# A hybrid encoder block on one core: wide half-K matmuls for queries and values, and a new order of weight chunks

## The chip, the cores and the metric

The kernel runs on one core of a Trainium2 chip. The metric is the device time of one execution, in microseconds (us). PE is TensorE, ACT ScalarE, DVE VectorE, POOL GpSimd and SP SyncE, which issues most DMAs. Each engine works through its own list of instructions in order and waits on semaphores.

## The reference

One layer on x of 2048 tokens by 1024, float32:

```python
h = rmsnorm(x, norm1_w)
qa, ka, va, qb, fb, ib, gb = split(h @ w_in)   # 512, 128, 128, 512, 512, 512, 512 columns
ya = sliding-window attention of qa, ka, va    # 8 query heads, 2 key heads, QK norm, partial rotary, sinks
yb = gated linear recurrence of qb, fb, ib     # 4 heads of 128, chunks of 64, rmsnorm, times silu(gb)
x  = x + concat(ya, yb) @ w_out
x  = x + (silu(h2 @ w_gate) * (h2 @ w_up)) @ w_down    # h2 = rmsnorm(x, norm2_w)
```

## The kernel before

Phase A computes everything up to `x + concat(ya, yb) @ w_out`; the feed-forward phase behind it (from about 840 us) isn't touched. A product of float32 operands is made of three passes (`three_passes`, L350 to L352): both operands are split into a high part in the matmul's format and the rest, and PE computes high x high, high x low and low x high.

Phase A takes the tokens in NB = 4 blocks of 512. For each block PE goes through twelve weight chunks (`CHUNKS`). A chunk is 1 MB (0.5 for F0 and F1): SP loads it into `w_stage`, ACT writes its high part (`split_hi`, L814), DVE the low part (`split_lo`, L1188). There are two buffers of each, used in turn, so a chunk is split while PE works on the one before. Heads of F, Q and G (names in `FIRST_HEAD`) are computed transposed, with the weights stationary and 512 tokens as moving columns, 24 matmuls a head. KV, QA0, QA1, I01 and I23 have the activations stationary and 256 weight columns moving, in four groups of 128 tokens, 24 matmuls a group. G's heads are cut in halves, `part` and `proj`. All of them write the banks `pj` in turn, and ACT reads each bank before its second next group.

Between the groups stand all other steps of the block, in an order written by hand (`block_steps`). Each entry `after(chunk, group, steps)` places steps behind a group, and every engine does its own share of each step in that one order, so a step that waits on an engine holds all that stands behind it there. The steps: `qn1`, `qn2` norm and rotary of queries and keys; `qT`, `kT` their transposes; `sc` scores of 128 tokens; `sm1` maximum (DVE) and exponentials (ACT) of one head group; `sm2` the division (DVE); `pt` transposes the probabilities on PE, and ACT copies them; `pv` times the values. For each of four recurrent heads: `ha` the log gate, `hb` its running sums (DVE) and then five exponentials (ACT), `hc` products (DVE), `att`, `kt` and `ds` matmuls and transposes with an ACT or DVE reading of their bank, `o` the output, `on1`, `on2` its norm, `yt` its transpose. `sq`, `n1a`, `n1b`, `xT` load, normalise and transpose the next block's x. The transposes of `qT`, `pt`, `kt`, `ds` and `yt` share two banks `tr`, used in turn: each waits until the bank's last content but one has been read. `sc` of t > 0 waits for the exponentials of t - 1.

`first_steps` are the two split steps of the next chunk. They stand ahead of group 0 of a chunk with heads and behind group 0 of the others, unless `block_steps` has placed them itself. What is left of the last heads of a block is done within KV and QA0 of the next (`LAST_HEAD`), and behind the last block within the output products (`out_steps`).

## Time and profile before

| | |
|---|---|
| median of 3 runs | 2134.61 us (2134.19 to 2135.76) |
| the profiled execution | 2135.83 us, of which the span from the first to the last instruction is 2134.0 |
| mean granted TensorE clock | 0.997 |
| PE busy in the span | 2099.1 us |

The profile is of one execution. A wait names the engine and the line that released it. Durations of neighbouring matmuls overlap, so the time of one in a stream is read from start to start. In a timeline the number in brackets is the engine's idle time before that row.

### The profile page before, as it was taken

The numbers are of one execution on the slowest core, as the hardware profiler recorded it, in microseconds if no ns is written. First come the engines' busy times: TensorE is split into PE (matmuls) and PEld (weight loads), VectorE is DVE, ScalarE is ACT, GpSimd is POOL, SyncE is SP. The second block draws the span as 40 slices with busy tenths as digits, with TensorE's granted clock in tenths as the row PEclk, the third lists the DMA queues.
The fourth block names the chain that finished last, engine by engine and source line by source line (L and its number), as shares of the span: only waits on it lengthen the run. The fifth ranks groups of instructions, "written<-read, shape, count | busy, mean of one in ns | idle before, by whom it ended". The sixth has DMA issues, their size and how long they took to land.

```text
span 2134.0 us, 28560 instructions
## 1 busy us (share of the span) xinstructions
PE 2099.1 (98%) x11128; PEld 1771.7 (83%) x11128; DVE 1377.9 (65%) x2034; ACT 886.0 (42%) x1490; POOL 105.5 (5%) x108
## 2 busy tenths in 40 slices
...
GB/s 280 130 75 124 165 80 85 199 80 104 134 86 216 204 263 203 163 133 145 152 158 173 96 146 168 217 143 178 151 144 178 170 253 185 205 179 167 181 134 90
DMA packets 176662, 338.10 MB, mean 158 GB/s; under 512 B 10448, under 2 KB 105936, under 8 KB 161552
## 3 DMA queue, kind: packets, MB, share of 16 engines
...
## 4 chain that ended last, share of the span: by engine, by line
PE 60%; DVE 0%; DVEq 0%; ACT 0%; issue 0%
PE b_bank_A L351 4%; PE b_bank_A L350 4%; PE b_bank_A L352 4%; PE b_bank_C L351 4%; PE b_bank_B L351 4%; PE b_bank_C L352 4%; PE b_bank_B L350 4%; PE b_bank_C L350 4%; PE b_bank_B L352 4%; PE b_hx_bank L1932 3%; PE b_hx_bank L1930 3%; PE b_hx_bank L1931 3%; PE b_bank_D L350 2%; PE b_bank_D L351 2%; PE b_bank_D L352 2%; PE b_hx_bank L1875 1%
## 5 line engine op out<-in xcount | busy, mean ns | idle before, releaser
L1816 ACT ACTIVATE b_s_hi<-b_s_stage 128x1408 fp32r<-128x1408 f32 x56 | 77.4, 1383 | 300.2 <-PE b_hx_bank L1932 143.7
L350 PE MATMUL a_pj<-a_w_hi,a_hT_hi 128*128 128x256 f32 x640 | 185.7, 290 | 1.5 <-DVE a_hT_lo L1202 1.5
L351 PE MATMUL a_pj<-a_w_lo,a_hT_hi 128*128 128x256 f32 x640 | 181.0, 283 | 0.0
L352 PE MATMUL a_pj<-a_w_hi,a_hT_lo 128*128 128x256 f32 x640 | 180.9, 283 | 0.0
L350 PE MATMUL a_pj<-a_hT_hi,a_w_hi 128*128 128x512 f32 x384 | 154.6, 403 | 6.4 <-ACT a_gT L871 6.0
L352 PE MATMUL a_pj<-a_hT_hi,a_w_lo 128*128 128x512 f32 x384 | 150.1, 391 | 0.0
L351 PE MATMUL a_pj<-a_hT_lo,a_w_hi 128*128 128x512 f32 x384 | 150.0, 391 | 0.0
L350 PE MATMUL b_bank_A<-b_h_hi_B,b_w_hi 128*128 128x512 f32 x352 | 137.9, 392 | 0.0
L351 PE MATMUL b_bank_A<-b_h_lo_B,b_w_hi 128*128 128x512 f32 x352 | 137.5, 391 | 0.0
L350 PE MATMUL b_bank_B<-b_h_hi_T,b_w_hi 128*128 128x512 f32 x352 | 137.3, 390 | 0.0
L352 PE MATMUL b_bank_A<-b_h_hi_B,b_w_lo 128*128 128x512 f32 x352 | 137.3, 390 | 0.0
L352 PE MATMUL b_bank_B<-b_h_hi_T,b_w_lo 128*128 128x512 f32 x352 | 137.0, 389 | 0.0
L351 PE MATMUL b_bank_B<-b_h_lo_T,b_w_hi 128*128 128x512 f32 x352 | 137.0, 389 | 0.0
L350 PEld LDWEIGHTS a_pj<-a_w_hi,a_hT_hi 128*128 128x128 f32 x640 | 122.5, 191 | 4.7 <-DVE a_hT_lo L1202 2.1
L351 PEld LDWEIGHTS a_pj<-a_w_lo,a_hT_hi 128*128 128x128 f32 x640 | 122.6, 192 | 0.0
L352 PEld LDWEIGHTS a_pj<-a_w_hi,a_hT_lo 128*128 128x128 f32 x640 | 122.5, 191 | 0.0
L1948 DVE TENSOR_TENSOR b_w_lo<-b_mixed_w,b_w_hi 128x1024 fp32r<-128x1024 f32 x88 | 107.5, 1222 | 21.6 <-ACT b_w_hi L1775 21.6
L1932 PE MATMUL b_hx_bank<-b_t_hi,b_s_lo 128*128 128x512 f32 x308 | 119.8, 389 | 0.0
L1930 PE MATMUL b_hx_bank<-b_t_hi,b_s_hi 128*128 128x512 f32 x308 | 119.8, 389 | 0.0
L1931 PE MATMUL b_hx_bank<-b_t_lo,b_s_hi 128*128 128x512 f32 x308 | 119.8, 389 | 0.0
L1188 DVE TENSOR_TENSOR a_w_lo<-a_w_stage,a_w_hi 128x2048 fp32r<-128x2048 f32 (+1 forms) x48 | 101.2, 2109 | 21.3 <-ACT a_w_hi L814 21.0
L1948 DVE TENSOR_TENSOR b_s_lo<-b_s_stage,b_s_hi 128x1408 fp32r<-128x1408 f32 x56 | 91.0, 1625 | 34.0 <-ACT b_s_hi L1816 33.0
...
## 6 DMA issues: line engine op xcount, KB each, us to landing
...
```

Source lines behind the costliest of these rows:

```text
L350: pe.matmul(out, stationary[0](k), moving[0](k), start=(k == 0 and not adds), stop=False, skip_group_check=adds)
L351: pe.matmul(out, stationary[0](k), moving[1](k), start=False, stop=False, skip_group_check=adds)
L352: last = pe.matmul(out, stationary[1](k), moving[0](k), start=False, stop=(k == ends), skip_group_check=adds)
L1188: dve.tensor_tensor(w_lo[s][:, :, 0:cols], w_stage[s][:, :, 0:cols], w_hi[s][:, :, 0:cols].bitcast(F32), ALU.subtract).then_inc(w_lo_ready ...
L1816: act.activation(f.s_hi[n % 2][:], f.s_stage[n % 2][:], ACT.Copy).then_inc(f.s_hi_ready, 1)
L1875: last = pe.transpose(f.hx_bank[part][:, k * 512 + t * P:k * 512 + (t + 1) * P], f.hx[q % 2][:, t, (2 * part + k) * P:(2 * part + k + 1) * ...
L1930: pe.matmul(out, s_hi[:, k, :], t_hi, start=(k == 0 and not adds), stop=False, skip_group_check=adds)
L1931: pe.matmul(out, s_hi[:, k, :], t_lo, start=False, stop=False, skip_group_check=adds)
L1932: last = pe.matmul(out, s_lo[:, k, :], t_hi, start=False, stop=(k == PAIRS_FF - 1), skip_group_check=adds)
L1948: dve.tensor_tensor(out, full, hi.bitcast(F32), ALU.subtract).then_inc(ready, 1)
```

## The change

QA0 and QA1, and I01 and I23, held 256 columns each with all of K. They become QAl and QAh, Il and Ih: 512 columns with the lower and the upper half of K. A group of them is 12 matmuls with 512 moving columns. The four groups of the lower half leave their sums in four banks (`pj` and `sc` for QA; `pvb`, `hb` and `pj` for I), the upper half adds to them, and ACT reads each bank once, 512 columns wide. The columns of qa are reordered on the way in, so that one read fits both halves. The first `pv` and the first `att` of a block wait for ACT to have read their bank.

The order of chunks changes: F23 now stands behind F1, Q01 behind it, and G01 behind Q23. The steps are placed anew among them. No split step is placed by hand any longer: all stand at the place of `first_steps`. The loading of chunks goes by lists of (block, chunk) pairs (`RAW`, `STAGED`), which hold every chunk of every block, as before. The scratch output of the squares of x gets memory of its own. The order of the steps around the first output products changes a little.

```diff
 
 
-CHUNKS = [("KV", 512, 256), ("QA0", 0, 256), ("QA1", 256, 256), ("F0", 1280, 128), ("F1", 1408, 128),
-          ("Q01", 768, 256), ("I01", 1792, 256), ("G01", 2304, 256), ("F23", 1536, 256), ("Q23", 1024, 256),
-          ("I23", 2048, 256), ("G23", 2560, 256)]
+CHUNKS = [("KV", 512, 256), ("QAl", 0, 512), ("QAh", 0, 512), ("F0", 1280, 128), ("F1", 1408, 128), ("F23", 1536, 256),
+          ("Q01", 768, 256), ("Il", 1792, 512), ("Ih", 1792, 512), ("Q23", 1024, 256), ("G01", 2304, 256), ("G23", 2560, 256)]
 NW = len(CHUNKS)
 FIRST_HEAD = {"F0": 0, "F1": 1, "F23": 2, "Q01": 0, "Q23": 2, "G01": 0, "G23": 2}
 HALF_CHUNKS = [n for n, c in enumerate(CHUNKS) if c[2] < WC]
 WHOLE_CHUNKS = [n for n in range(NW) if n not in HALF_CHUNKS]
+K_HALF = {"QAl": 0, "Il": 0, "QAh": 1, "Ih": 1}
+RAW = [(b, n) for b in range(NB) for n in range(NW)]
+STAGED = [[chunk for chunk in RAW if chunk[1] % 2 == s] for s in range(2)]
+
+
...
-def block_steps():
+def block_steps(b):
 
     at = {}
 
@@ -89,38 +108,38 @@
         at.setdefault((name, group), []).extend(steps)
 
     after("KV", 3, ("vmix",))
-    after("QA1", 0, ("qn1", 0))
-    after("QA1", 1, ("qn1", 1))
-    after("QA1", 2, ("qn1", 2), ("qn2", 0))
-    after("QA1", 3, ("qn1", 3))
-    after("F0", 0, ("qn2", 1), ("split_hi", CHUNK_AT["Q01"]), ("split_lo", CHUNK_AT["Q01"]), ("qn2", 2))
+    after("QAh", 0, ("qn1", 0))
+    after("QAh", 1, ("qn1", 1))
+    after("QAh", 2, ("qn1", 2), ("qn2", 0))
+    after("QAh", 3, ("qn1", 3))
+    after("F0", 0, ("qn2", 1), ("qn2", 2))
     after("F1", 0, ("qn2", 3))
-    after("Q01", 0, ("qT", 0), ("qT", 1), ("kT",), ("qT", 2), ("qT", 3))
-    after("Q01", 1, ("sc", 0), ("sm1", 0), ("sm1", 1))
-    after("I01", 0, ("ha", 0), ("split_hi", CHUNK_AT["G01"]))
-    after("I01", 1, ("sm2", 0), ("sm2", 1), ("sc", 1), ("split_lo", CHUNK_AT["G01"]))
-    after("I01", 2, ("pt", 0), ("pt", 1), ("sm1", 2), ("sm1", 3), ("hb", 0))
-    after("I01", 3, ("sm2", 2), ("sm2", 3), ("pv", 0), ("sc", 2))
-    after("G01", 0, ("pt", 2), ("pt", 3), ("sm1", 4), ("sm1", 5), ("xload",), ("hc", 0), ("ha", 1))
-    after("G01", 1, ("sm2", 4), ("sm2", 5), ("pv", 1))
-    after("G01", 2, ("pt", 4), ("pt", 5), ("sc", 3), ("att", 0), ("kt", 0), ("split_hi", CHUNK_AT["F23"]), ("sm1", 6), ("sm1", 7), ("split_lo", CHUNK_AT["F23"]), ("hb", 1))
-    after("G01", 3, ("ds", 0, 0), ("ds", 0, 1), ("sm2", 6), ("sm2", 7), ("pv", 2), ("hc", 1))
-    after("F23", 1, ("o", 0), ("on1", 0), ("kt", 1), ("pt", 6), ("pt", 7), ("ha", 2), ("sq", 0))
-    after("Q23", 0, ("pv", 3), ("on2", 0), ("hb", 2), ("split_lo", CHUNK_AT["I23"]), ("ds", 1, 0), ("ds", 1, 1), ("att", 1), ("sq", 1))
-    after("Q23", 1, ("yt", 0), ("hc", 2), ("sq", 2))
-    after("I23", 0, ("o", 1), ("on1", 1), ("ha", 3), ("sq", 3))
-    after("I23", 1, ("on2", 1), ("n1a",), ("kt", 2), ("hb", 3), ("split_lo", CHUNK_AT["G23"]))
-    after("I23", 2, ("yt", 1), ("att", 2), ("hc", 3))
-    after("I23", 3, ("n1b", 0), ("n1b", 1), ("n1b", 2), ("n1b", 3))
-    after("G23", 0, ("ds", 2, 0), ("ds", 2, 1), ("split_hi", NW), ("split_lo", NW))
-    after("G23", 1, ("xT", 0), ("xT", 1))
-    after("G23", 2, ("o", 2), ("on1", 2), ("kt", 3), ("xT", 2), ("xT", 3))
-    after("G23", 3, ("xT", 4), ("xT", 5), ("xT", 6), ("xT", 7))
-
-    placed = [step for group in at.values() for step in group if step[0].startswith("split")]
+    after("F23", 0, ("qT", 0), ("qT", 1), ("kT",))
+    after("F23", 1, ("qT", 2), ("qT", 3))
+    after("Q01", 0, ("sc", 0), ("xload",))
+    after("Q01", 1, ("sm1", 0), ("sm1", 1))
+    after("Il", 0, ("ha", 0))
+    after("Il", 1, ("sm2", 0), ("sm2", 1), ("sc", 1), ("hb", 0))
+    after("Il", 2, ("pt", 0), ("pt", 1), ("sm1", 2), ("sm1", 3))
+    after("Il", 3, ("hc", 0), ("ha", 1))
+    after("Ih", 0, ("sm2", 2), ("sm2", 3), ("sc", 2), ("hb", 1))
+    after("Ih", 1, ("pv", 0), ("kt", 0))
+    after("Ih", 2, ("pt", 2), ("pt", 3), ("att", 0), ("sm1", 4), ("sm1", 5))
+    after("Ih", 3, ("hc", 1), ("sm2", 4), ("sm2", 5), ("sq", 0))
+    after("Q23", 0, ("pv", 1), ("ds", 0, 0), ("ds", 0, 1), ("sc", 3), ("sq", 1))
+    after("Q23", 1, ("pt", 4), ("pt", 5), ("o", 0), ("on1", 0), ("sm1", 6), ("sm1", 7), ("ha", 2))
+    after("G01", 0, ("sm2", 6), ("sm2", 7), ("pv", 2), ("on2", 0), ("kt", 1), ("hb", 2))
+    after("G01", 1, ("pt", 6), ("pt", 7), ("att", 1), ("sq", 2), ("hc", 2))
+    after("G01", 2, ("yt", 0), ("ds", 1, 0), ("ds", 1, 1), ("pv", 3), ("ha", 3), ("hb", 3))
+    after("G01", 3, ("kt", 2), ("sq", 3), ("n1a",), ("hc", 3))
+    after("G23", 0, ("o", 1), ("on1", 1), ("n1b", 0), ("n1b", 1), ("n1b", 2), ("n1b", 3))
+    after("G23", 1, ("on2", 1), ("xT", 0), ("xT", 1))
+    after("G23", 2, ("att", 2), ("yt", 1), ("ds", 2, 0), ("ds", 2, 1), ("xT", 2), ("xT", 3))
+    after("G23", 3, ("kt", 3), ("xT", 4), ("xT", 5), ("xT", 6), ("xT", 7))
+
     steps = []
     for n in range(NW):
-        first_steps = [part for part in (("split_hi", n + 1), ("split_lo", n + 1)) if part not in placed]
+        first_steps = [("split_hi", n + 1), ("split_lo", n + 1)] if n + 1 < NW or b < NB - 1 else []
         for g in range(chunk_groups(n)):
             if g == 0 and chunk_groups(n) < TT:
                 steps += first_steps
@@ -135,9 +154,8 @@
     return steps
 
 
-STEPS = block_steps()
-LAST_HEAD = {("KV", 0): (("on2", 2), ("ds", 3, 0), ("ds", 3, 1)), ("KV", 1): (("att", 3),),
-             ("KV", 2): (("yt", 2), ("o", 3), ("on1", 3)), ("KV", 3): (("on2", 3),), ("QA0", 0): (("yt", 3),)}
+LAST_HEADS = {("KV", 0): (("o", 2), ("on1", 2)), ("KV", 1): (("on2", 2), ("ds", 3, 0), ("ds", 3, 1)), ("KV", 2): (("att", 3),),
+              ("KV", 3): (("yt", 2), ("o", 3), ("on1", 3)), ("QAl", 0): (("on2", 3),), ("QAl", 1): (("yt", 3),)}
...
-    after(0, 0, ("att", 3), ("a_lo", 0, 4), ("t_hi", 4), ("t_lo", 4))
-    after(0, 1, ("yt", 2), ("o", 3), ("on1", 3), ("t_hi", 5), ("t_lo", 5), ("a_load", 1))
-    after(0, 2, ("t_hi", 6), ("on2", 3), ("a_lo", 0, 5), ("n2w_load",))
-    after(0, 3, ("yt", 3), ("t_lo", 6), ("a_lo", 0, 6))
+    after(0, 0, ("on2", 2), ("ds", 3, 0), ("ds", 3, 1), ("a_lo", 0, 4), ("t_hi", 4), ("t_lo", 4))
+    after(0, 1, ("att", 3), ("yt", 2), ("t_hi", 5), ("t_lo", 5))
+    after(0, 2, ("o", 3), ("on1", 3), ("a_load", 1), ("a_lo", 0, 5), ("n2w_load",))
+    after(0, 3, ("on2", 3), ("t_hi", 6), ("a_lo", 0, 6))
+    after(0, 4, ("yt", 3), ("t_lo", 6))
...
-    junk = put("a_junk", [P, D], BF16, at=prob_at)
+    junk = put("a_junk", [P, D], BF16, at=mem.at + 2 * D * 4)
...
+    def group_bank(n, g):
+
+        name = chunk_name(n)
+        if name[0] == "I":
+            return (pvb, hb, pj[0], pj[1])[g]
+        return (pj + sc)[g] if name[:2] == "QA" else pj[(GROUPS_TO[n] + g) % 2]
+
+    bank_free = {"KV": ((-1, g_ready, 3), (-1, g_ready, 4), (0, kv_ready, 1), (0, kv_ready, 2)),
+                 "QAl": ((0, kv_ready, 3), (0, kv_ready, 4)), "F0": ((0, qa_ready, 1),), "F1": ((0, qa_ready, 2),),
+                 "F23": ((0, f_ready, 1), (0, f_ready, 2)), "Q01": ((0, f_ready, 3), (0, f_ready, 4)),
+                 "Il": (None, None, (0, q_ready, 1), (0, q_ready, 2)), "Q23": ((0, i_ready, 3), (0, i_ready, 4)),
+                 "G01": ((0, q_ready, 3), (0, q_ready, 4)), "G23": ((0, g_ready, 1), (0, g_ready, 2))}
+
+    def wait_bank_free(pe, b, n, g):
+
+        free = bank_free.get(chunk_name(n), ())
+        if g < len(free) and free[g] is not None and b + free[g][0] >= 0:
+            back, read, count = free[g]
+            pe.wait_ge(read.sem, read.upto(b + back, count))
 
...
                 if kind == "split_hi":
-                    split(b, step[1])
-                elif kind == "proj":
+                    split(*((b, step[1]) if step[1] < NW else (b + 1, 0)))
+                elif kind == "proj" and chunk_name(step[1]) not in ("QAl", "Il"):
...
-                    elif name[:2] == "QA":
-
-                        half = int(name[2])
-                        act.activation(qk[:, g, half:N_Q:2, :], ps[:, 0:WC].rearrange("p (s d) -> p s d", d=HD), ACT.Copy).then_inc(qa_ready.sem, 1)
+                    elif name == "QAh":
+                        act.activation(qk[:, g, 0:N_Q, :], ps[:].rearrange("p (s d) -> p s d", d=HD), ACT.Copy).then_inc(qa_ready.sem, 1)
                     else:
-                        c0 = WC * (name == "I23")
-                        act.activation(i_nat[:, g, c0:c0 + WC], ps[:, 0:WC], ACT.Copy).then_inc(i_ready.sem, 1)
+                        act.activation(i_nat[:, g, :], ps[:], ACT.Copy).then_inc(i_ready.sem, 1)
...
+                    elif name in K_HALF:
+                        first_k = K_HALF[name] * (KT // 2)
+                        wide_hi, wide_lo = (part[s][:].rearrange("p a c -> p (a c)") for part in (w_hi, w_lo))
+                        last = three_passes(pe, bank[:], still,
+                                            (lambda k: wide_hi[:, (k - first_k) * 512:(k - first_k + 1) * 512],
+                                             lambda k: wide_lo[:, (k - first_k) * 512:(k - first_k + 1) * 512]), range(first_k, first_k + KT // 2))
...
                     wait_from(pe, yA_ready.sem, yA_ready.upto(b, t))
+                    if t == 0:
+                        pe.wait_ge(i_ready.sem, i_ready.upto(b, 1))
...
                     pe.wait_ge(hb_read.sem, hb_read.upto(b, h))
+                    if h == 0:
+                        pe.wait_ge(i_ready.sem, i_ready.upto(b, 2))
```

## Rows read from the trace of the kernel before

**Rows 1.** The page, part 1: busy time of each engine

```profile
PE 2099.1 (98%) x11128; PEld 1771.7 (83%) x11128; DVE 1377.9 (65%) x2034; ACT 886.0 (42%) x1490; POOL 105.5 (5%) x108
```

**Rows 2.** Waits of PE: total us, times, longest us

```profile
PE a_pj L350 <- ACT a_gT L871: 6.0, 4, 1.5
PE a_tr L1092 <- ACT a_k_nat L942: 3.2, 4, 0.8
PE b_hx_bank L1875 <- PEq L2120: 3.0, 1, 3.0
...
PE a_pj L350 <- DVE a_hT_lo L1202: 1.5, 3, 0.5
```

**Rows 3.** Timeline of PE, second block: start, duration, instruction, idle before

```profile
219.37 0.40 PE L350 MATMUL a_pj<-a_hT_hi,a_w_hi 128*128 128x512 f32 x1
...
250.84 0.71 PE L1083 MATMUL a_sc<-a_kT_even,a_qT 64*128 64x128 f32 x8
...
287.21 0.50 PE L350 MATMUL a_pj<-a_hT_hi,a_w_hi 128*128 128x512 f32 x1 [1.51 <-ACT a_gT L871]
...
453.69 0.50 PE L350 MATMUL a_pj<-a_hT_hi,a_w_hi 128*128 128x512 f32 x1 [1.48 <-ACT a_gT L871]
```

**Rows 4.** Timeline of PE: first and last of 163 narrow, of 55 wide

```profile
21.57 0.28 PE L350 MATMUL a_pj<-a_w_hi,a_hT_hi 128*128 128x256 f32 x1
...
41.01 0.28 PE L350 MATMUL a_pj<-a_w_hi,a_hT_hi 128*128 128x256 f32 x1
...
222.12 0.39 PE L350 MATMUL a_pj<-a_hT_hi,a_w_hi 128*128 128x512 f32 x1
...
234.36 0.39 PE L350 MATMUL a_pj<-a_hT_hi,a_w_hi 128*128 128x512 f32 x1
```

**Rows 5.** Timeline of ACT, from Q01's second head on

```profile
243.92 0.60 ACT L869 ACTIVATE a_q_h<-a_pj 128x512 f32<-128x512 f32 x1 [3.52 <-PE a_pj L352]
244.54 1.28 ACT L848 ACT_TABLE_LOAD   x1
...
250.46 1.93 ACT L814 ACTIVATE a_w_hi<-a_w_stage 128x2048 fp32r<-128x2048 f32 x1
...
255.55 1.09 ACT L932 ACTIVATE a_probT<-a_tr 128x512 f32<-128x512 f32 x2
256.52 0.21 ACT L924 ACTIVATE a_sink_e<-a_sink_less 128x4 f32<-128x4 f32 x1
...
259.88 0.63 ACT L900 ACTIVATE a_q_in<-a_t_a 128x512 f32<-128x512 f32 x1 [0.28 <-DVE a_k_end L1291]
...
262.26 0.36 ACT L881 ACTIVATE a_i_nat<-a_pj 128x256 f32<-128x256 f32 x1
```

**Rows 6.** Timeline of DVE: qn2, split, sm1, hb, sm2

```profile
223.76 0.83 DVE L1258 TENSOR_TENSOR a_qk<-a_qk,a_q_rs 128x640 f32<-128x640 f32 x1
...
225.83 0.33 DVE L1272 TENSOR_TENSOR a_qk<-a_rope_u,a_rope_v 128x160 f32<-128x160 f32 x1
...
252.42 2.29 DVE L1188 TENSOR_TENSOR a_w_lo<-a_w_stage,a_w_hi 128x2048 fp32r<-128x2048 f32 x1 [1.41 <-ACT a_w_hi L814]
254.63 0.68 DVE L1309 TENSOR_REDUCE a_top<-a_sc 128x4 f32<-128x512 f32 x1
...
256.93 0.42 DVE L1281 TENSOR_SCALAR a_f_gate<-a_f_gate 128x512 f32<-128x512 f32 x1
...
259.76 0.15 DVE L1318 TENSOR_TENSOR a_denom<-a_denom,a_sink_e 128x4 f32<-128x4 f32 x1
...
261.94 0.68 DVE L1309 TENSOR_REDUCE a_top<-a_sc 128x4 f32<-128x512 f32 x1
```

**Rows 7.** Timeline of DVE: seven steps of the state, scaling of x

```profile
282.95 2.88 DVE L1337 SCALAR_TENSOR_TENSOR a_state<-a_state,a_decay,a_tr 128x128 f32<-128x128 f32 x7
...
330.06 2.73 DVE L1197 TENSOR_SCALAR a_x_in<-a_x_in,a_x_rs 128x1024 f32<-128x1024 f32 x4
```

**Rows 8.** Stretch 843 to 848 us: engines' busy us, clock, DMA share, GB/s

```profile
843.00:848.00 5.00, 2.55 (x12) 2.15 (x11) 4.85 (x7) 3.11 (x3) 1.17 (x2) 0.50 0.89 356
```

More of the change, by code:

```diff
@@ L58, with raw_count, staged_count, next_staged @@
 WHOLE_CHUNKS = [n for n in range(NW) if n not in HALF_CHUNKS]
+K_HALF = {"QAl": 0, "Il": 0, "QAh": 1, "Ih": 1}
+RAW = [(b, n) for b in range(NB) for n in range(NW)]
+STAGED = [[chunk for chunk in RAW if chunk[1] % 2 == s] for s in range(2)]
+def raw_count(b, n):
+    return RAW.index((b, n)) + 1
+def staged_count(b, n):
+    return STAGED[n % 2].index((b, n)) + 1
+def next_staged(b, n):
+    same = STAGED[n % 2]
+    at = same.index((b, n)) + 1
+    return same[at] if at < len(same) else None
 def chunk_name(n):
@@ L247, in plan @@
         extra = out_prepared() if b == NB - 1 else out_weight_sums(b)
-        for step in STEPS:
+        for step in block_steps(b):
             if b == NB - 1 and of_next_block(step):
@@ L254, in plan @@
                 if b > 0:
-                    steps += [(b - 1, late) for late in LAST_HEAD.get(place, ())]
+                    steps += [(b - 1, late) for late in LAST_HEADS.get(place, ())]
                 steps += [(b, early) for early in extra.get(place, ())]
@@ L693, in _ @@
             if kind == "split_lo":
-                n = step[1]
-                if b * NW + n + 2 < NB * NW:
-                    sp.wait_ge(w_lo_ready.sem, w_lo_ready.upto(b, n))
-                    load(n + 2)
+                of, n = (b, step[1]) if step[1] < NW else (b + 1, 0)
+                sp.wait_ge(w_lo_ready, raw_count(of, n))
+                following = next_staged(of, n)
+                if following is not None:
+                    load(following[1])
             elif kind == "pv":
```

111 lines of the change are left out of this document (52 added, 59 removed).

## The prediction, made before the run

> **What bounds the kernel now.** I read the page first: TensorE (PE) is busy for 98% of the span [rows 1]. Then PE's own waits [rows 2]. In the stage that the change touches (four blocks of 512 tokens, up to about 690 us) only three places make PE wait, and they return once per block: 6.0 us in 4 times for a G bank that ScalarE (ACT) has not read, 3.2 in 4 for `k_nat`, 1.5 in 3 for `hT_lo`. That is 1.5 + 0.8 + 0.5 = 2.8 us a block. The same wait in two blocks following one another gives the period, 453.69 - 287.21 = 166.5 us [rows 3]. So a block is 163.7 us of PE work and 2.8 of waiting. There are two ways to move the time: fewer nanoseconds per matmul, or another amount of waiting. The second depends on whether the two in-order queues that feed PE, ACT and VectorE (DVE), stay ahead, and I read those from the timeline [rows 5 to 7].
>
> **What the wide matmuls give.** Per block, QA0, QA1, I01 and I23 are 4 chunks x 4 groups x 8 tiles x 3 passes = 384 matmuls of 256 columns. They become 192 of 512 columns (4 half-K chunks x 4 groups x 4 x 3). Start to start, 162 narrow ones take 41.01 - 21.57 = 19.44 us, 120.0 ns each; 54 wide ones take 234.36 - 222.12 = 12.24 us, 226.7 ns each [rows 4]. Two narrow less one wide is 13.3 ns; the rounding of the starts allows 12 to 14. I take 12.5: 192 x 12.5 = 2.4 us a block, 9.6 in all. The Trainium skill (TensorE: Matmul & The Clock Gate, section Back-to-back issue gap) prices a matmul at its columns over 2.4 GHz plus some 2.5 ns. By that the saving would be 768 x 2.5 ns, about 2 us, as an estimate; the trace disagrees, with more than 13 ns over the column time, and the trace decides. ACT also reads 8 banks of 512 columns instead of 16 of 256, and loads tables less often; ACT doesn't hold PE by its total, so this counts only inside the chains below. SP's queue carries the same 12 weight loads per block, each released by the split two chunks earlier, so more than 10 us ahead of its use: 0.
>
> **What the new order does.** Before, F23 stands behind G01, and six chunks lie between the scores of the first tokens and the block's end. Now F23 stands ahead of Q01 and five are left, while the attention and gate steps (`sm`, `pt`, `pv`, `ha`, `hb`, `hc`, `ds`) are the same. The same DVE and ACT work has 10.9 us less matmul time above it. And the hand-placed splits are gone: each `split_hi`/`split_lo` now stands right behind group 0 (or ahead of it, for F, Q, G), in front of steps that PE needs sooner.
>
> I walk one block with E = 0 where the second group of Q01 ends. A half-K group is 12 x 0.227 = 2.73 us, an F/Q/G head 5.46. On ACT [rows 5]: reading a bank 0.6, table 1.3, two `sm1` 3.1 (256.52 to 259.60), high split 1.9, two `pt` 1.0, `hb` 2.4. On DVE [rows 6, 7]: low split 2.2, two `sm1` 2.3, `hb` 2.85, two `sm2` 2.2, `ds` 3.5 (one copy and eight steps of the state), four `n1b` 2.7. PE's small steps: a score step is two runs of matmuls, 1.1 us [rows 3], the others 0.4 to 2.
>
> (1) *F23's weights, 0.9.* DVE is held by `qn2` 1, `qn2` 2 ahead of the low split of F23. `qn2` 1 starts at 223.76 now, 4.4 us behind the start of F0 at 219.37 [rows 3, 6]; two of 2.4 (this one ends at 226.16) and a split of 2.2 end 11.8 after F0's start; F0 and F1 last 10.9.
> (2) *`pt` 0 and 1, 2.4.* ACT reads the bank and loads the table until 2.0, `sm1` to 5.1, log to 5.6, split of Ih to 7.6. DVE: low split to 9.8, only then `sm2` 0 and 1, ready at 11.0 and 12.1. PE has done Il 0 to 2 and a score step at 9.4.
> (3) *`sc` 2, 3.5.* `hb` 0 now stands ahead of the `pt` copies. DVE's part starts at 12.0, ACT's at 14.9 to 17.3; `pt` copies to 18.4, `sm1` 2 and 3 to 21.5. PE, which resumed at 12.6, is there at 18.1.
> (4) *`pt` 3, 1.7.* Its bank is free when ACT has copied `kt` 0. ACT is in `hb` 1 (25.7 to 28.2), then in the split of Q23 (to 30.1), and copies `kt` 0 at 31.8. PE is there at 30.2.
> (5) *`pt` 6 and 7, 5.5.* By 52.9 PE has finished `o` 0; squares, table and `sm1` 6, 7 take ACT to 58.6, log and split of G23 to 61.1. DVE's low split ends at 63.3, `sm2` 6 and 7 at 64.5 and 65.6. PE wants them at 59.9.
> (6) *`yt` 0 and `ds` 1, 4.1 + 0.9.* `hb` 2 starts on DVE at 66.2, on ACT at 69.1; table, G01's bank, `pt` 6 and 7 until 74.5. The transpose bank of `yt` 0 waits for them; PE is there at 69.9. `ds` 1 then waits for DVE to read `yt` 0.
> (7) *First x transposes, 9.1.* `hb` 3 begins behind `ds` 1, ends on ACT at 86.7; table, bank, `kt` 2, last square to 90.3; then low split of the next KV to 94.5 and `n1b` to 97.4. PE has finished G23's first head at 88.3.
> (8) *Tail, 1.9.* `ds` 2 waits for `yt` 1 (1.4), and the 0.5 of `hT_lo` stays.
>
> That is 30.0 us of waits a block. The old 2.8 and the 2.4 of wide matmuls go off: +24.8 for each of the first three blocks, 74.4. The last block prepares no next x: without (7) and (8), 19.0 of waits, less 2.3 and 2.4, +14.3. Its output stage gets operands later; I bound that by 0 and 3 and take 0, since nothing later than (6) is queued there. Sum: +88.7. Against this execution's own 2135.8 us (span 2134.0 and 1.8 around it) that is 2224.5. The median is 1.2 below that execution: 2223.
>
> The bounds of the stalls: below, each could vanish if an earlier one already let the queues catch up, since they share their work; the smallest set that I can't see vanish is (1) to (3), 6.8 a block, +1.6 net. Above, all eight and the clock.
>
> **Rivals.**
> *Part of it.* The queues recover behind the first stalls, and the waits (5) to (7) shrink. For it: ACT and DVE are busy 42% and 65% over the whole span. Against it: (5) to (7) are chains, not totals. Without (7) and (8) the sum is 88.7 - 33.0, 2190 us; with (1) to (3) alone some 2140.
> *The other sign: the splits and steps stay ahead.* The place is the first `pt`: if `sm2` 1 is ready by 9.4 instead of 12.1, `hb` 0 and everything behind it come earlier by as much, and the order runs as smoothly as the old one. Then the 9.6 us of wide matmuls are gained, and up to 4 x 2.8 of the old waits, which sat at G01 and F23: 2114 to 2125. For it: before, only 2.8 us a block were lost. Against it: before, `sm2` 0 and 1 stood ahead of the split (they were done 1.4 us before DVE got its operand [rows 6]) and `hb` 0 behind the copies; both are turned round.
> *The clock falls too.* After 3.0 us without work at the change of stages [rows 2] and a further 2.4 the granted clock is 0.50, 1.2 GHz, in the stretch of 5 us around it [rows 8]. Stalls (5) and (7) are longer. If 8 us behind (7) run at half speed, 4 us are lost in three blocks: 2235; behind (5) too, 2250. The Trainium skill (the same page, section HAM oscillation — how this bites in real kernels) says that idle gaps between bursts bring the clock down. By that rule the clock would fall behind (5) and (7) in every block: 2235 to 2250. I give it less, because where ACT and DVE set the pace a slower PE hides in its own waits, and PE sets it only behind (7).
>
> **How the numbers follow.** Forecast 0.60, part of it 0.20, the other sign 0.12, the clock 0.08. The likeliest alone is 2190 to 2240. The range 2150 to 2250 leaves out the other sign and the smallest partial case, together some 0.17. Within 0.2% (about what a measurement of this kernel can tell) lies a sliver of the partial case, 0.03. Slower 0.85, faster 0.12.
>
> **What would show it.** Period of a block 190 us or so instead of 166.5; among PE's waits `a_prob` on DVE (2 and 5), `a_sc` on ACT's `a_prob` (3), the transposes of `a_x_in` on DVE's `a_x_in` as the longest single wait (7). Wide matmuls 227 ns start to start. If PE's waits stay under 4 us a block, the walk is wrong and the other sign holds. If the waits (2) and (3) are there and (5) to (7) are not, it is the partial case.

## The result and the profile after

The changed kernel takes 2233.3 us (2232.87 to 2233.5, 4 runs), the kernel before 2135.07 us (2134.19 to 2135.76, 4 runs) on the same chip: ratio 1.046, 95% interval 1.0442 to 1.0478. That is 98.2 us slower; the forecast was 2223, 10 us less.

Page, part 1, and the clock line of part 2, of the changed kernel:

```profile
PE 2116.9 (95%) x10360; PEld 1746.8 (78%) x10360; DVE 1380.3 (62%) x2034; ACT 854.8 (38%) x1438; POOL 107.9 (5%) x108
...
PEclk9989998999999999999999999999999999999999
```

Against [rows 1]: PE runs 768 matmuls fewer and is busy 17.8 us longer. The span grew from 2134.0 to 2231.7, 97.7 us; span less busy time is PE's idle time, 34.9 before and 114.8 now. So 79.9 us are more idle time and 17.8 us more busy time. The clock line shows an 8 in two of its first seven slices.

Waits of PE after (total us, times, longest us). The numbers of steps in brackets below are those of the prediction:

```profile
PE a_sc L1024 <- DVE a_x_in L1230: 28.0, 3, 9.7
PE a_tr L1123 <- DVE a_prob L1355: 24.5, 13, 4.2
...
PE a_sc L1114 <- ACT a_prob L955: 11.0, 4, 3.2
PE a_tr L1166 <- DVE a_yH L1386: 8.7, 8, 1.3
PE a_tr L1185 <- ACT a_probT L961: 8.5, 4, 2.5
PE a_pj L369 <- DVE a_w_lo L1221: 3.5, 4, 0.9
...
PE a_tr L1123 <- ACT a_k_nat L971: 1.1, 1, 1.1
```

The wait for G's bank, 6.0 us in [rows 2], is gone, and `k_nat` is down from 3.2 to 1.1. In their place are the waits ahead of the transposes of `a_x_in` (step 7), `a_prob` (2 and 5), `a_sc` on ACT's `a_prob` (3), `a_yH` (6 and 8), `a_probT` (6), and F23's weights (1).

The timeline of PE in the second block after, with the places that wait:

```profile
257.14 0.50 PE L369 MATMUL a_pj<-a_hT_hi,a_w_hi 128*128 128x512 f32 x1 [0.86 <-DVE a_w_lo L1221]
...
293.61 0.66 PE L1123 MATMUL a_tr<-ident,a_prob 128*128 128x128 f32 x4 [1.36 <-DVE a_prob L1355]
294.70 0.65 PE L1123 MATMUL a_tr<-ident,a_prob 128*128 128x128 f32 x4 [0.44 <-DVE a_prob L1355]
...
304.00 1.18 PE L1114 MATMUL a_sc<-a_kT_even,a_qT 64*128 64x128 f32 x8 [3.16 <-ACT a_prob L955]
...
346.97 1.11 PE L1123 MATMUL a_tr<-ident,a_prob 128*128 128x128 f32 x4 [4.15 <-DVE a_prob L1355]
348.42 1.11 PE L1123 MATMUL a_tr<-ident,a_prob 128*128 128x128 f32 x4 [0.34 <-DVE a_prob L1355]
...
356.85 0.63 PE L1185 MATMUL a_tr<-ident,a_y_nat 128*128 128x128 f32 x4 [2.47 <-ACT a_probT L961]
358.41 1.86 PE L1166 MATMUL a_tr<-a_i_nat,a_k_nat 64*128 64x128 f32 x16 [0.94 <-DVE a_yH L1386]
...
381.98 1.94 PE L1024 MATMUL a_sc<-ident,a_x_in 128*128 128x128 f32 x8 [8.76 <-DVE a_x_in L1230]
383.57 0.78 PE L369 MATMUL a_pj<-a_hT_hi,a_w_hi 128*128 128x512 f32 x1
...
387.54 1.05 PE L1146 MATMUL a_hb<-a_q_in,a_f_gate 128*128 128x128 f32 x8
...
450.71 0.50 PE L369 MATMUL a_pj<-a_hT_hi,a_w_hi 128*128 128x512 f32 x1 [0.87 <-DVE a_w_lo L1221]
```

From F23 to F23 is 450.71 - 257.14 = 193.6 us, where 166.5 was the period before [rows 3]. The 12 wide matmuls from 383.57 on take 3.97 us, not 12 x 0.227 = 2.7. Seven stretches of the windows view of the same kernel show the lower clock (busy us of PE, PEld, DVE, ACT, POOL; clock; DMA share; GB/s):

```profile
303.00:306.00 3.00, 2.00 (x17) 1.78 (x17) 2.70 (x9) 1.95 (x8) 0.00 (x0) 0.68 0.00 0
306.00:309.00 3.00, 3.00 (x12) 2.44 (x11) 2.09 (x3) 0.80 (x2) 0.00 (x0) 0.75 0.00 0
...
345.00:348.00 3.00, 1.03 (x4) 0.71 (x4) 2.35 (x7) 0.00 (x0) 0.00 (x0) 0.51 0.44 63
348.00:351.00 3.00, 2.67 (x14) 2.59 (x13) 2.93 (x5) 0.00 (x0) 0.00 (x0) 0.50 0.89 355
...
378.00:381.00 3.00, 0.00 (x0) 0.00 (x0) 3.00 (x5) 0.00 (x0) 1.73 (x1) 0.50 0.31 44
381.00:384.00 3.00, 2.02 (x9) 2.05 (x10) 1.60 (x4) 0.73 (x2) 0.21 (x1) 0.50 0.73 306
384.00:387.00 3.00, 3.00 (x10) 2.35 (x10) 1.33 (x2) 0.64 (x1) 0.00 (x0) 0.67 0.00 0
```

PE does nothing from 378 to 381, the granted clock is 0.50 (1.2 GHz), and it is still 0.50 to 0.67 when the work is back. The same happens around the wait of 4.15 us that ends at 346.97, and for a shorter time behind that of 3.16 us which ends at 304.00.

In step (2) the splits of Ih stand ahead of `sm2`. DVE stands idle for 9.07 us until ACT has written the high part, and only behind the low part does it write the probabilities that PE transposes at 293.61 and 294.70:

```profile
290.17 2.29 DVE L1221 TENSOR_TENSOR a_w_lo<-a_w_stage,a_w_hi 128x2048 fp32r<-128x2048 f32 x1 [9.07 <-ACT a_w_hi L846]
...
292.86 0.69 DVE L1355 TENSOR_TENSOR a_prob<-a_prob,a_denom 128x512 f32<-128x512 f32 x1
...
293.95 0.69 DVE L1355 TENSOR_TENSOR a_prob<-a_prob,a_denom 128x512 f32<-128x512 f32 x1
```

Step (7) is the longest wait. While PE idles from 378 to 381, ACT does nothing either and DVE is busy without a gap. DVE's timeline of that wait:

```profile
374.17 0.17 DVE L1225 TENSOR_SCALAR a_ss<-a_ss 128x4 f32<-128x4 f32 x1 [6.17 <-ACT a_junk L852]
374.25 0.69 DVE L1329 TENSOR_TENSOR a_q_in<-a_q_in,a_q_h 128x512 f32<-128x512 f32 x1
...
376.22 0.68 DVE L1333 TENSOR_TENSOR a_q_h<-a_q_h,a_t_b 128x512 f32<-128x512 f32 x1
376.82 2.28 DVE L1221 TENSOR_TENSOR a_w_lo<-a_w_stage,a_w_hi 128x2048 fp32r<-128x2048 f32 x1
...
379.10 2.74 DVE L1230 TENSOR_SCALAR a_x_in<-a_x_in,a_x_rs 128x1024 f32<-128x1024 f32 x4
```

DVE had stood idle for 6.17 us until ACT's last square. `n1a`, the four products of `hc` 3, the low split of the next KV and the four `n1b` then follow without a gap until 381.84; PE starts at 381.98. It is a chain, not a full engine: DVE is busy for 62% of the span.

### The profile page after: what moved, and what is told of

It is laid out like the page before. It is cut to its first block, busy times and chain, and to the rows that moved or that the text cites. A ratio compares the mean times of both kernels' runs of the same rounds, so it can differ in the third digit from the quotient of the medians.

```text
span 2231.7 us, 26963 instructions
## 1 busy us (share of the span) xinstructions
PE 2116.9 (95%) x10360; PEld 1746.8 (78%) x10360; DVE 1380.3 (62%) x2034; ACT 854.8 (38%) x1438; POOL 107.9 (5%) x108
## 4 chain that ended last, share of the span: by engine, by line
PE 57%; DVE 0%; DVEq 0%; ACT 0%; issue 0%
PE b_bank_C L371 4%; PE b_bank_B L371 4%; PE b_bank_A L371 4%; PE b_bank_C L369 4%; PE b_bank_B L369 4%; PE b_bank_A L369 4%; PE b_bank_A L370 4%; PE b_bank_B L370 4%; PE b_bank_C L370 4%; PE b_hx_bank L1964 3%; PE b_hx_bank L1963 3%; PE b_hx_bank L1965 3%; PE b_bank_D L369 2%; PE b_bank_D L371 2%; PE b_bank_D L370 2%; PE b_hx_bank L1908 1%
## 5 line engine op out<-in xcount | busy, mean ns | idle before, releaser
L1981 DVE TENSOR_TENSOR b_w_lo<-b_mixed_w,b_w_hi 128x1024 fp32r<-128x1024 f32 x88 | 107.5, 1222 | 21.5 <-ACT b_w_hi L1808 21.5
L1888 ACT ACTIVATE b_gate<-b_u 128x512 f32<-128x512 f32 x44 | 27.8, 633 | 196.7 <-DVE b_u L2132 196.6
L1871 ACT ACTIVATE b_s<-b_bank_C 128x512 f32<-128x512 f32 x44 | 26.4, 599 | 200.1 <-PE b_bank_C L371 200.1
L369 PEld LDWEIGHTS a_pj<-a_hT_hi,a_w_hi 128*128 128x128 f32 x384 | 74.3, 193 | 23.9 <-DVE a_w_lo L1221 5.1
L369 PE MATMUL a_pj<-a_w_hi,a_hT_hi 128*128 128x256 f32 (+1 forms) x256 | 90.3, 353 | 1.5 <-DVE a_hT_lo L1235 1.5
L370 PE MATMUL a_pj<-a_w_lo,a_hT_hi 128*128 128x256 f32 (+1 forms) x256 | 86.7, 339 | 0.0
L371 PE MATMUL a_pj<-a_w_hi,a_hT_lo 128*128 128x256 f32 (+1 forms) x256 | 86.7, 339 | 0.0
```

The source lines that it names most:

```text
L369: pe.matmul(out, stationary[0](k), moving[0](k), start=(k == 0 and not adds), stop=False, skip_group_check=adds)
L370: pe.matmul(out, stationary[0](k), moving[1](k), start=False, stop=False, skip_group_check=adds)
L371: last = pe.matmul(out, stationary[1](k), moving[0](k), start=False, stop=(k == ends), skip_group_check=adds)
L1871: act.activation(f.s5[:], f.bank["C"][:], ACT.Copy).then_inc(f.s5_ready, 1)
L1888: act.activation(f.gate[1][:], f.u2[:], ACT.Silu).then_inc(f.silu_ready[1], 1)
L1981: dve.tensor_tensor(out, full, hi.bitcast(F32), ALU.subtract).then_inc(ready, 1)
```

## The experiments

There are ten kernels. A ratio is to the kernel before on the same chip. A difference to the change is one between chips, on which the medians of the kernel before differ by up to 0.9 us. The first two ask whether the wide format or the order makes the loss.

**Format taken back, order kept.**

```diff
-CHUNKS = [("KV", 512, 256), ("QAl", 0, 512), ("QAh", 0, 512), ("F0", 1280, 128), ("F1", 1408, 128), ("F23", 1536, 256),
-          ("Q01", 768, 256), ("Il", 1792, 512), ("Ih", 1792, 512), ("Q23", 1024, 256), ("G01", 2304, 256), ("G23", 2560, 256)]
+CHUNKS = [("KV", 512, 256), ("QA0", 0, 256), ("QA1", 256, 256), ("F0", 1280, 128), ("F1", 1408, 128), ("F23", 1536, 256),
+          ("Q01", 768, 256), ("I01", 1792, 256), ("I23", 2048, 256), ("Q23", 1024, 256), ("G01", 2304, 256), ("G23", 2560, 256)]
...
-        if name[0] == "I":
-            return (pvb, hb, pj[0], pj[1])[g]
-        return (pj + sc)[g] if name[:2] == "QA" else pj[(GROUPS_TO[n] + g) % 2]
+        return pj[(GROUPS_TO[n] + g) % 2]
```

> The changed kernel with the format alone taken back: QA and I in narrow chunks of 256 columns over all of K, in the two projection banks, in the places where the wide halves stand; chunk order, splits and steps as after the change. If the order of chunks and steps makes the loss (the forecast's theory), the same waits return and the 9.6 us of the wide matmuls go: 2233 + 10 = about 2243 us, 2238 to 2252, with a first x transpose that still waits 8 us or more per block. If the wide groups make it (four banks shared with scores and attention, reads of the sums only behind the second half), most of the 98 us goes: 2135 to 2170 us.

Measured: 2239.72 us (2239.05 to 2240.97), ratio to before 1.0491 (1.0475 to 1.0507). The longest wait is the same, and `a_prob` is within 1 us:

```profile
PE a_sc L1028 <- DVE a_x_in L1230: 26.1, 3, 9.7
PE a_tr L1127 <- DVE a_prob L1355: 25.1, 15, 4.2
```

The order of chunks and steps makes the loss, not the format. Inside that order the format brings 6.4 us, not 9.6. The waits are not quite the same: the score step waits 3.0 us instead of 11.0, and PE waits 7.2 us for ACT to read I's sums (`a_i_nat`), which it did not do in the change.

**Only QA wide, everything else as before.** Against the kernel before:

```diff
-CHUNKS = [("KV", 512, 256), ("QA0", 0, 256), ("QA1", 256, 256), ("F0", 1280, 128), ("F1", 1408, 128),
+CHUNKS = [("KV", 512, 256), ("QAl", 0, 512), ("QAh", 0, 512), ("F0", 1280, 128), ("F1", 1408, 128),
           ("Q01", 768, 256), ("I01", 1792, 256), ("G01", 2304, 256), ("F23", 1536, 256), ("Q23", 1024, 256),
```

> The kernel before, with QA alone as wide K halves over four banks; order of chunks, splits and steps as before. By the pitches, 2 chunks x 4 groups x 12 wide matmuls = 96 matmuls a block less, at 12.5 ns, are 1.2 us a block, 4.8 in all: 2130.3 us, 2128 to 2132, and PE's waits as before (about 2.8 us a block). If the gap between two matmuls were worth only 2.5 ns each, some 1 us, not to be told from no change. If reading only behind the second half, from banks shared with the scores, brings waits of its own, it is slower than before: 2137 or more.

Measured: 2130.56 us (2129.86 to 2131.18, 11 runs) against 2135.55: ratio 0.9977 (0.9969 to 0.9986). PE's two main waits of [rows 2] stay at 6.0 and 3.2 us. 5.0 us for 384 matmuls less is 13.0 ns each.

The next six ask where the loss sits, whether its places depend on each other, and what the clock costs.

**One split and one hb put back.**

```diff
-    after("Il", 0, ("ha", 0))
-    after("Il", 1, ("sm2", 0), ("sm2", 1), ("sc", 1), ("hb", 0))
-    after("Il", 2, ("pt", 0), ("pt", 1), ("sm1", 2), ("sm1", 3))
+    after("Il", 0, ("ha", 0), ("split_hi", CHUNK_AT["Ih"]))
+    after("Il", 1, ("sm2", 0), ("sm2", 1), ("sc", 1), ("split_lo", CHUNK_AT["Ih"]))
+    after("Il", 2, ("pt", 0), ("pt", 1), ("sm1", 2), ("sm1", 3), ("hb", 0))
```

> The changed kernel with the steps in Il alone as before the change: the splits of Ih placed by hand behind sm2 0 and 1, and hb 0 behind sm1 2 and 3. The forecast counted 5.9 us a block of waits there (2 and 3), so if the places of this one split and this one hb make them: 2233 - 24 = about 2209 us. If what counts is the chain of ACT and DVE between two products of PE, and this edit only changes which member of it is late (a walk of the queues has pt 0 and sc 2 free of waits, but pv 0 then waits some 2 us for I's sums and pt 3 some 5 for the copy of kt 0), the time stays within 4 us of 2233.

Measured: 2239.87 us (2237.77 to 2242.78), ratio to before 1.0488 (1.0474 to 1.0502), 6.6 slower than the change: outside of the 4 that I had allowed and far from 2209. Its waits of PE:

```profile
PE a_tr L1124 <- DVE a_prob L1356: 17.2, 6, 4.2
PE a_tr L1124 <- ACT a_k_nat L972: 15.9, 4, 4.7
...
PE a_pv L1136 <- ACT a_i_nat L911: 7.7, 4, 1.9
```

`a_prob` lost 7.3 us and the wait of the score step on ACT, 11.0 before, no longer appears; `a_k_nat` took 14.8 more and I's sums 7.7. The longest of the two, 4.7 and 1.9 us, are the "some 5" and "some 2" of the expectation. The wait moved to the next users of the same chain: this edit buys nothing.

**All splits of the kernel before at their default place.**

```diff
-    after("I01", 0, ("ha", 0), ("split_hi", CHUNK_AT["G01"]))
-    after("I01", 1, ("sm2", 0), ("sm2", 1), ("sc", 1), ("split_lo", CHUNK_AT["G01"]))
+    after("I01", 0, ("ha", 0))
+    after("I01", 1, ("sm2", 0), ("sm2", 1), ("sc", 1))
...
-    placed = [step for group in at.values() for step in group if step[0].startswith("split")]
+    placed = []
```

> The kernel before with nothing changed but the splits that were placed by hand: all stand at their default place, ahead of a chunk's first group (F, Q, G) or behind it (I), as the change has it. Narrow chunks, old order. If placing of splits against steps is a cause by itself, waits of 9 to 11 us a block appear (at pt 0, pt 4, yt 1): 2135 + 36 to 44 = about 2175 us. If the loss needs the new order of chunks or the moved steps, under 2145 us.

Measured: 2180.68 us (2180.29 to 2183.57), ratio 1.0213 (1.0199 to 1.0227): 45 us lost with narrow chunks in the old order, about 1 us above the 36 to 44 expected. New waits of PE:

```profile
PE a_tr L1092 <- DVE a_prob L1322: 17.3, 15, 2.8
...
PE a_tr L1150 <- DVE a_y_nat L1347: 10.9, 5, 2.8
```

These are the same splits and no other work, only behind other steps. PE's busy time is 2115.8 us where it was 2099.1 with the same 11128 matmuls, so 16.7 of the 45 us are not waits.

**One knot loosened: the first softmax and gate.**

```diff
-    after("Q01", 0, ("sc", 0), ("xload",))
-    after("Q01", 1, ("sm1", 0), ("sm1", 1))
-    after("Il", 0, ("ha", 0))
-    after("Il", 1, ("sm2", 0), ("sm2", 1), ("sc", 1), ("hb", 0))
-    after("Il", 2, ("pt", 0), ("pt", 1), ("sm1", 2), ("sm1", 3))
-    after("Il", 3, ("hc", 0), ("ha", 1))
+    after("Q01", 0, ("sc", 0), ("xload",), ("ha", 0), ("sm1", 0), ("hb", 0), ("sm1", 1))
+    after("Q01", 1, ("sm2", 0), ("sm2", 1), ("hc", 0))
+    after("Il", 1, ("pt", 0), ("sc", 1), ("pt", 1))
+    after("Il", 2, ("sm1", 2), ("sm1", 3))
+    after("Il", 3, ("ha", 1))
```

> The changed kernel with one knot alone loosened, at its first place: hb 0, sm2 0 and 1 and hc 0 stand ahead of Il instead of behind its second group, and sc 1, pt 0 and pt 1 one group later. If the waits 2, 3 and 4 of the forecast come from this knot, they go (5.0 us of waits a block and the lower clock around them) and the waits 5 to 8 stay as they are, because they have their own chains: 2233 - 4 x 6 or 7 = 2205 to 2212 us. If all waits are one backlog that is only handed on (ACT and DVE too slow for the block), the 5 us return at pt 6 or xT 0 and the time stays within 5 us of 2233. If the waits 5 to 7 hang on this knot too, it falls below 2190.

Measured: 2207.86 us (2207.74 to 2207.99), 25.4 faster than the change. Waits of PE:

```profile
PE a_sc L1024 <- DVE a_x_in L1230: 24.0, 3, 8.4
PE a_tr L1123 <- DVE a_prob L1355: 17.1, 6, 4.2
```

The score step's 11.0 us are gone, and so is `k_nat`'s 1.1; PE now waits 6 times for `a_prob`, not 13 (steps 2 to 4). The later waits stay, that for `a_probT` with 11.4 us instead of 8.5, so the ones that went were no backlog that is handed on.

**The next x scaled first.**

```diff
-    after("Q23", 1, ("pt", 4), ("pt", 5), ("o", 0), ("on1", 0), ("sm1", 6), ("sm1", 7), ("ha", 2))
+    after("Q23", 1, ("pt", 4), ("pt", 5), ("o", 0), ("on1", 0), ("sm1", 6), ("sm1", 7), ("ha", 2), ("sq", 2), ("sq", 3))
-    after("G01", 1, ("pt", 6), ("pt", 7), ("att", 1), ("sq", 2), ("hc", 2))
+    after("G01", 1, ("pt", 6), ("pt", 7), ("att", 1), ("n1a",), ("hc", 2))
-    after("G01", 3, ("kt", 2), ("sq", 3), ("n1a",), ("hc", 3))
-    after("G23", 0, ("o", 1), ("on1", 1), ("n1b", 0), ("n1b", 1), ("n1b", 2), ("n1b", 3))
+    after("G01", 3, ("n1b", 0), ("n1b", 1), ("n1b", 2), ("n1b", 3), ("kt", 2), ("hc", 3))
+    after("G23", 0, ("o", 1), ("on1", 1))
```

> The changed kernel with the scaling of the next x ahead of the third and fourth gate: squares 2 and 3 behind Q23, n1a behind pt 7, the four n1b straight behind G01. The wait of the first x transposes (28.0 us in three blocks) should vanish. If waits of PE in this kernel were each on their own, 2233 - 28 and the clock behind it, 6 or so, gives about 2200 us. If the same queues owe the work elsewhere, the forecast's theory, half or more comes back: pt 6 waits 2 to 3 us more behind the two squares, att 2 3.5 for hc 2: 2233 - 12 - 4 = 2215 to 2222 us.

Measured: 2219.32 us (2217.28 to 2221.77), 14.0 faster. Waits of PE:

```profile
PE a_tr L1124 <- DVE a_prob L1356: 31.7, 13, 6.6
...
PE a_hb L1147 <- DVE a_y_nat L1381: 6.7, 4, 2.6
```

The 28.0 us for `a_x_in` are gone. PE waits 7.2 us more for `a_prob`, up to 6.6 at a time behind the two squares, and `a_hb` 5.6 more for `a_y_nat`: 13 of the 28 come back. This place does share its queues with its neighbours.

**Both edits at once**, the two diffs above together.

> The changed kernel with both single edits at once: that of the early run (25.4 us faster than the change) and that of the x_first run (14.0 us faster). If the knots are independent of each other, each a chain of ACT and DVE at its own place, the gains add: 2233 - 39 = 2194 us, 2190 to 2198. If both draw on one backlog, the second adds little: 2203 to 2208. If the early one gives the queues room that x_first can use (pt 6 waited 6.6 us there), under 2188.

Measured: 2191.0 us (2188.74 to 2191.99), 42.3 faster than the change, where 25.4 + 14.0 = 39.4. The gains of these two places add, to within 3 us.

**The price of the clock.** In the wait ahead of the first x transpose PE gets work that nobody needs:

```diff
                 pe.wait_ge(yA_ready.sem, yA_ready.upto(b, TT))
+                for i in range(32):
+                    pe.matmul(sc[0][:], w_hi[1][:, i % KT, 0:P], hT_hi[:, hT_slot(b, i % KT), :], start=True, stop=True)
```

> The changed kernel with 32 matmuls more of 512 columns in each of three blocks, whose result nobody reads, in the wait ahead of the first x transpose (about 7.3 us of work at 227 ns in a wait of 8.8 to 9.7 us). They take no time of their own unless they outlast the wait. If the granted clock of 0.50 to 0.67 in the 5 us behind that wait comes from the idle wait and costs PE time on the path, the clock stays at 1.00 there and the kernel is 3 to 7 us faster: 2226 to 2230 us. If the slower PE there is hidden behind ACT and DVE, or the clock falls whatever PE does, within 1 us of 2233. If the added work holds the transposes up, slower.

Measured: 2229.49 us (2228.46 to 2233.57), 3.8 faster by the medians. Two of the five runs took as long as the change (2233.3 and 2233.6), and the two intervals against before (1.0434 to 1.0462 here) overlap, so the time alone does not carry it. The profiled execution, the fastest of the five, shows what happens at the wait, in the timeline of PE and one window:

```profile
380.05 1.09 PE L1024 MATMUL a_sc<-ident,a_x_in 128*128 128x128 f32 x8 [0.81 <-DVE a_x_in L1232]
380.90 0.48 PE L369 MATMUL a_pj<-a_hT_hi,a_w_hi 128*128 128x512 f32 x1
...
383.75 1.05 PE L1148 MATMUL a_hb<-a_q_in,a_f_gate 128*128 128x128 f32 x8
```

```profile
378.00:381.00 3.00, 2.19 (x15) 1.66 (x14) 2.59 (x5) 0.25 (x1) 1.37 (x1) 1.00 0.94 289
```

The clock stays at 1.00, the eight transposes take 1.09 us instead of 1.94, and from the first transpose to `att` 2 are 3.70 us instead of 5.56: 1.9 us a block. So the clock at this place fell because PE stood idle, and the 1.9 us are on the path: this execution's span is 5.0 us shorter, 2226.7 against 2231.7.

The last two ask whether the order of chunks is at fault, and look for a faster kernel.

**Order of chunks, format and default splits as in the change; the steps placed anew.** Its first half:

```diff
...
+    after("Q01", 0, ("sc", 0), ("sm1", 0), ("xload",), ("hb", 0), ("sm1", 1))
+    after("Q01", 1, ("sm2", 0), ("sm2", 1), ("hc", 0))
+    after("Il", 1, ("pt", 0), ("sc", 1), ("pt", 1))
+    after("Il", 2, ("sm1", 2), ("sq", 0), ("sm2", 2), ("sm1", 3), ("ha", 1))
+    after("Ih", 2, ("pv", 0), ("kt", 0), ("pt", 2), ("sc", 2), ("sm2", 3), ("pt", 3), ("hb", 1), ("sm1", 4), ("sm1", 5))
+    after("Ih", 3, ("sm2", 4), ("hc", 1), ("sq", 1), ("sm2", 5))
+    after("Q23", 0, ("ds", 0, 0), ("ds", 0, 1))
...
```

> The changed kernel with the order of its chunks, its wide formats and its default splits untouched, and only the steps (softmax, gates, state, squares and scaling of x) put in other places: the first score and softmax step and hb 0 directly behind Q01's first group, sm2 straight behind sm1, squares of x from Il on, o and yt later. If the loss is in the placing of the steps against the splits, a walk of the queues leaves about 1 us of waits a block: four blocks at about 160 us instead of 193, so some 2233 - 4 x 30 = 2105 to 2120 us, below the kernel before. If the order of chunks leaves too little matmul time above the attention work (F23 ahead of Q01), no placing mends it and it stays over 2180 us.

Measured: 2119.79 us (2118.46 to 2120.8), ratio to before 0.9927 (0.9914 to 0.9941), at the upper end of what was expected. Page part 1, two of its waits of PE, and the first product of the second and of the third block on the timeline:

```profile
PE 2090.5 (99%) x10360; PEld 1733.0 (82%) x10360; DVE 1379.1 (65%) x2034; ACT 886.9 (42%) x1462; POOL 107.2 (5%) x108
```

```profile
PE a_hb L1169 <- DVE a_att_m L1358: 3.3, 2, 2.3
...
PE a_pj L365 <- DVE a_w_lo L1217: 0.7, 4, 0.2
```

```profile
175.25 0.39 PE L365 MATMUL a_pj<-a_w_hi,a_hT_hi 128*128 128x256 f32 x1 [0.49 <-DVE a_hT_lo L1231]
...
336.85 0.39 PE L365 MATMUL a_pj<-a_w_hi,a_hT_hi 128*128 128x256 f32 x1 [0.49 <-DVE a_hT_lo L1231]
```

The period is 161.6 us. The list of steps runs four times, and writing it anew takes 32.0 of 193.6 us out of each.

**All wide, F23 where it stood before, steps placed anew.**

```diff
-CHUNKS = [("KV", 512, 256), ("QAl", 0, 512), ("QAh", 0, 512), ("F0", 1280, 128), ("F1", 1408, 128), ("F23", 1536, 256),
-          ("Q01", 768, 256), ("Il", 1792, 512), ("Ih", 1792, 512), ("Q23", 1024, 256), ("G01", 2304, 256), ("G23", 2560, 256)]
+CHUNKS = [("KV", 512, 256), ("QAl", 0, 512), ("QAh", 0, 512), ("F0", 1280, 128), ("F1", 1408, 128), ("Q01", 768, 256),
+          ("Il", 1792, 512), ("Ih", 1792, 512), ("F23", 1536, 256), ("Q23", 1024, 256), ("G01", 2304, 256), ("G23", 2560, 256)]
...
+    after("Il", 0, ("split_hi", CHUNK_AT["Ih"]))
+    after("Il", 1, ("sm2", 0))
+    after("Il", 2, ("pt", 0), ("hb", 0), ("sm2", 1), ("split_lo", CHUNK_AT["Ih"]), ("sc", 1), ("sm1", 2), ("pt", 1))
...
```

> All of QA and I as wide K halves over four banks as in the change, but F23 left where it stood before the change, behind the I chunks (KV, QAl, QAh, F0, F1, Q01, Il, Ih, F23, Q23, G01, G23), and the steps placed anew for that order, as in the reordered run for the new one. The wide matmuls give 9.6 us, the old waits of up to 2.8 us a block may go: 2114 to 2126 us. If the new order of chunks is by itself no better and no worse, it lies within 6 us of the 2119.8 us of the reordered run. If F23's early place is the merit of the change, it is 2130 or more; if it is its fault, under 2112.

Measured: 2114.56 us (2113.74 to 2115.14), ratio to before 0.9902 (0.9886 to 0.9919), the fastest of all. Its page and the same two places:

```profile
PE 2085.9 (99%) x10360; PEld 1729.3 (82%) x10360; DVE 1379.0 (65%) x2034; ACT 877.1 (42%) x1454; POOL 107.6 (5%) x108
```

```profile
177.03 0.39 PE L366 MATMUL a_pj<-a_w_hi,a_hT_hi 128*128 128x256 f32 x1 [0.50 <-DVE a_hT_lo L1232]
...
338.05 0.39 PE L366 MATMUL a_pj<-a_w_hi,a_hT_hi 128*128 128x256 f32 x1 [0.50 <-DVE a_hT_lo L1232]
```

A block takes 161.0 us, 0.6 less than with F23 early, and at the first product of the fourth block the two kernels are still within 0.7 us of each other (499.09 here, 498.45 there). So, as far as two lists written by hand can tell, the order of the chunks is worth next to nothing in these blocks once the steps fit it. This kernel also places some splits by hand again, which the reordered one does not. The 5.2 us between the two arise behind that product, where the reordered kernel waits 3.3 us for `a_att_m`. Against before, this kernel is 21.0 us faster: 9.6 are the wide matmuls, and the waits for G's bank (6.0) and `k_nat` (3.2) no longer appear. The remaining 2.2 are not traced.

## Why the prediction was right, and where its parts were not

**What bounds it, and the direction: right.** The waits are there at seven of the eight steps, with the releasers named, the order and not the format makes the loss, and the format alone is worth what the pitches said.

**Wide matmuls, 9.6 us: right.** QA alone gave 5.0 of 4.8 expected. The Trainium skill (TensorE: Matmul & The Clock Gate, section Back-to-back issue gap) would have given about 1 us for this run, as an estimate from its 2.5 ns; this case's 13.0 ns do not agree. In the new order, where ACT and DVE set the pace, only 6.4 us of the 9.6 arrived.

**The eight waits: right in place, too large in sum.** This is the second block, us. The two columns on the right are the time at which PE is there and the time at which it is released, from the end of Q01 (282.6 in the trace).

| step | wait, forecast | wait, measured | there / released, forecast | there / released, measured |
|---|---|---|---|---|
| (1) F23's weights | 0.9 | 0.86 | | |
| (2) `pt` 0 and 1 | 2.4 | 1.80 | 9.4 / 11.0 | 9.6 / 11.0 |
| (3) `sc` 2 | 3.5 | 3.16 | 18.1 / 21.5 | 18.2 / 21.4 |
| (4) `pt` 3 | 1.7 | none | 30.2 / 31.8 | no wait |
| (5) `pt` 6 and 7 | 5.5 | 4.49 | 59.9 / 64.5 | 60.2 / 64.4 |
| (6) `yt` 0 and `ds` 1 | 4.1 + 0.9 | 2.47 + 0.94 | 69.9 / 74.0 | 71.8 / 74.2 |
| (7) x transposes | 9.1 | 8.76 | 88.3 / 97.4 | 90.6 / 99.4 |
| (8) tail | 1.4 + 0.5 | 1.22 + 0.50 | | |
| sum | 30.0 | 24.2 | | |

Up to (6) ACT and DVE release PE within 0.3 us of the forecast. Two slips in the walk show here. In (1) its own terms, 4.4 and two of 2.4 and 2.2, end at 11.4 and not at 11.8, which makes a wait of 0.5; that 0.86 was measured is luck, because `qn2` 1 starts 4.75 us behind F0 and not 4.4. In (7) it left out that `hc` 3 stands on DVE between the last square and the low split: ACT's high split ends at 375.95, and DVE begins the low one at 376.82, 0.9 us later.

**No clock in the sum: wrong, and partly hidden by the waits.** The forecast net was 98.3 us of waits less 9.6. Measured are 79.9 us more of idle time and 17.8 more of busy time. So the idle time was 18.4 less than forecast, and the busy time 27.4 more. That the 27.4 is no other work is shown by the reordered kernel: it runs the same 10360 matmuls in 2090.5 us instead of 2116.9. How much of it is the clock can be estimated from the windows view in steps of 1 us up to 860 us: PE's busy time in each, times what its granted clock lacks of 1.00, adds up to 26.7 us in the changed kernel, 3.9 in the one before and 5.5 in the reordered one. So some 21 to 23 us are the lower clock; the other 4 to 6 are not traced.

The table shows how the slower work hides. The walk had PE arrive at each place at full speed. Behind (3) the score step and the twelve matmuls take 5.64 us (304.00 to 309.64) instead of the 1.1 + 2.73 of the walk, at a clock of 0.68 to 0.75. The 1.8 us are gone at (5), and so is the wait (4). Behind (5), with the clock at 0.50, PE reaches (6) 1.9 us late and waits 1.6 us less. The forecast had said so of the rival: where ACT and DVE set the pace a slower PE hides in its own waits. The forecast let it show only behind (7), but it also shows ahead of (7): `hb` 3 stands behind `ds` 1, whose sixteen matmuls take 1.86 us at the lower clock and 1.16 at full speed (390.25), and the release of (7) comes 2.0 us late, of which `hc` 3 is 0.9. Behind (7) I had put 4 us a block for the rival; the filler shows 1.9. The Trainium skill (the same page, section HAM oscillation — how this bites in real kernels) says that idle gaps between bursts bring the clock down; the trace agrees, 0.50 in the wait of 8.76 us and 1.00 there when the wait was filled.

In sum 27.4 - 18.4 = 9.0 us (of spans, 97.7 against 88.7) stand above the forecast: 5.2 in the three periods from F23 to F23 (79.6 us longer than before, 74.4 forecast) and 3.8 in the rest, the last block and the output stage. No run divides them between the clock, `hc` 3 and the rest. That the forecast came within 10 us is in part luck, since two errors of 18 and 27 us have opposite signs. The outcome is the likeliest case with a part of the third rival, in the upper part of the range given for the likeliest.

**The reasons for the waits.** The forecast named two: five chunks instead of six as cover, and splits at their default place ahead of steps that PE needs. The first does not decide: with F23 early and the steps placed anew there are no such waits. The second alone, in the old order, costs 45 us; but with the very same default splits the reordered kernel loses nothing. Neither a split nor a chunk is in the wrong place by itself. What costs, as the timelines of (2) and (7) have it, is a list in which DVE or ACT does something long (a split of 2.2 us, a gate of 2.4 to 2.9) between two links of a chain that PE waits for. A small edit can hand the wait on, as the run with one split and one `hb` put back shows; loosening a whole knot gained 25.4 us, and two of them 42.3 of the 98. That nothing less than a new list gets all of it back was not shown. How the 98 us divide over the two reasons was not separated further.

**The rivals.** Part of it: the queues did not recover behind (1) to (3), and when (2) to (4) were removed (5) to (8) stayed. The other sign needed `sm2` 1 ready earlier; the run with the first knot loosened did that and still lost at the later places. Its time, 2114 to 2125 us, was reached only by the two lists written anew.
